# Two attention scores issued one behind the other on the two halves of TensorE's rows

## The reference

```python
def attend(qb):                      # 128 queries of each of 8 heads, head width 64
    s = einsum('bkgqd,bksd->bkgqs', qb, kh)      # 128 x 256 scores, no mask
    p = softmax(s, axis=-1)
    return einsum('bkgqs,bksd->bkgqd', p, vh)
o = lax.map(attend, q_blocks)        # 2 blocks of queries
o = rms_norm_2(o, out_gain)
mixed = concatenate([o_gla, o], -1)
h = h + mixed @ w_out                # then norm, router, top 2 of 64 experts, final norm
```

## Time and profile before

| | us |
|---|---|
| median of 3 runs | 1407.85 (1407.63 to 1408.08) |
| the profiled execution, its own time | 1395.12 |
| its span, first to last instruction | 1393.3 |
| PE busy | 1048.4 (75%) |
| DVE busy | 479.4 (34%) |
| ACT busy | 283.5 (20%) |

### The profile page before, as it was taken

One profiled execution on the slowest core, in us unless ns is written; L12 is line 12 of the kernel. 1 busy time (PEld: TensorE's weight loads), 2 busy tenths in 40 slices (PEclk: granted clock), 3 DMA queues, 4 the chain that ended last, 5 costly groups with the idle time before them and its releaser, 6 DMA issues.

```text
span 1393.3 us, 21666 instructions
## 1 busy us (share of the span) xinstructions
PE 1048.4 (75%) x9215; PEld 660.8 (47%) x9215; DVE 479.4 (34%) x1052; ACT 283.5 (20%) x610; POOL 36.1 (3%) x34
## 2 busy tenths in 40 slices
PE   8999999999999886675656766676665756757566
PEld 6857777878765542342323323233332423324232
DVE  4456785787954431221202212021120211212122
ACT  4334342544822111010001001010010110100000
POOL 0000101011102000000000000000000000000000
PEclk9999999999999998898889889798897988888898
DMA  8462255403575599999999999999999999999995
GB/s 308 136 242 70 70 203 181 155 31 131 183 313 236 211 377 426 425 428 425 427 426 425 428 426 425 428 426 425 428 427 425 428 425 427 427 425 427 427 424 239
DMA packets 69808, 463.75 MB, mean 333 GB/s; under 512 B 6722, under 2 KB 15108, under 8 KB 36356
## 3 DMA queue, kind: packets, MB, share of 16 engines
q1 hardware_dynamic: 68976, 460.48, 80.7%
q10 hardware_dynamic: 788, 2.66, 0.5%
HBM read 462.07 MB, written 1.05 MB: 332 GB/s over the span
## 4 chain that ended last, share of the span: by engine, by line
DMA 46%; PE 43%; DVE 6%; ACT 1%; issue 1%; SPq 1%; POOL 0%; DVEq 0%; ACTq 0%
DMA ring<-in_w_up 46%; PE bank L2226 14%; PE bank L1813 13%; PE bank L1796 5%; PE bank L1768 3%; PE bank L1842 2%; PE bank L1862 2%; PE bank L2246 1%; PE bank L1883 1%; SPq L552 1%; DVE ring_lo L1115 1%; PE bank L2300 1%; DVE ring_lo L1120 1%; PE bank L2208 1%; DMA res<-in_x 0%
## 5 line engine op out<-in xcount | busy, mean ns | idle before, releaser
L2226 PE MATMUL bank<-ring,expert_area 128*32 128x256 f32 x3968 | 323.3, 492 | 219.3 <-DMA ring<-in_w_up 219.0
L2226 PEld LDWEIGHTS bank<-ring,expert_area 128*32 128x32 f32 x3968 | 149.5, 137 | 385.8 <-DMA ring<-in_w_up 239.7
L1813 PE MATMUL bank<-ring_lo,xt_hi 128*128 128x512 f32 (+3 forms) x576 | 182.8, 386 | 0.6 <-DVE small L1305 0.4
L1650 DVE TENSOR_TENSOR expert_area<-expert_area,bank 128x128 f32<-128x128 f32 x64 | 18.3, 285 | 469.6 <-ACT expert_area L1008 469.6
L1008 ACT ACTIVATE expert_area<-bank 128x128 f32<-128x128 f32 x64 | 17.8, 278 | 618.0 <-PE bank L2226 618.0
L2246 PE MATMUL bank<-ring,consts 128*32 128x256 f32 x2016 | 121.8, 382 | 27.9 <-DVE consts L1652 27.9
L1813 PEld LDWEIGHTS bank<-ring_lo,xt_hi 128*128 128x128 f32 x576 | 104.1, 188 | 20.6 <-issue 3.7
L2246 PEld LDWEIGHTS bank<-ring,consts 128*32 128x32 f32 x2016 | 62.2, 109 | 69.2 <-DVE consts L1652 20.1
L1813 PE MATMUL bank<-ring_lo,xt_lo 128*128 128x512 f32 (+2 forms) x240 | 91.2, 380 | 0.0
L1796 PE MATMUL bank<-ring,xt 128*128 128x384 f32 (+1 forms) x192 | 75.7, 541 | 1.4 <-DVE xt L1079 0.8
L1656 DVE COPY consts<-bank 32x256 f32<-32x256 f32 x63 | 26.5, 421 | 132.7 <-PE bank L2246 132.7
(11 more groups left out here) (286 smaller groups left out, 1149.1 us busy)
## 6 DMA issues: line engine op xcount, KB each, us to landing
ring<-in_w_down SPq DMA_DIRECT2D x62, 2048.0 KB, 24.8
ring<-in_w_gate SPq DMA_DIRECT2D x61, 2048.0 KB, 18.3
ring<-in_w_up SPq DMA_DIRECT2D x60, 2048.0 KB, 22.8
ring<-in_moba_w_kv SPq DMA_DIRECT2D x4, 2048.0 KB, 8.0
ring<-in_moba_w_in SPq DMA_DIRECT2D x4, 2048.0 KB, 8.6
ring<-in_w_in SPq DMA_DIRECT2D x3, 2048.0 KB, 7.8
ring<-in_mla_w_uq SPq DMA_DIRECT2D x4, 1152.0 KB, 5.6
ring<-in_mla_w_o SPq DMA_DIRECT2D x2, 2048.0 KB, 7.9
```

What stands on the lines that cost most here:

```text
L1813: last = nc.tensor.matmul(dst, x[at], w[:, c, :], start=(piece == 0 and c == 0 and w is hi and x is xt_hi), stop=(piece == 1 and c == 3 an ...
L2226: last = nc.tensor.matmul(bank[2][SLOTS * j:SLOTS * j + SLOTS, 0:256], picked[:, c, SLOTS * i:SLOTS * i + SLOTS], both[:, :, c, j // 2, j ...
```

## The change

The body that issues a unit's scores becomes a function `score(u)`, unchanged in what it waits for and issues. For kinds "a" and "b" it is called at the same place as before. For kind "g" it is called at even steps only, for unit u and then at once for unit u+1. Every other instruction and wait stays where it was.

```diff
             def attention(kind, units, depth, scores, values, beside):
+                def score(u):
+                    h, tile = unit_of(kind, u)
+                    keys = keys_of(kind, tile)
+                    dst = score_bank_of(kind, u)
+                    if u >= 4:
+                        pe.wait_ge(probs_done, UNIT0[kind] + score_bank_before(kind, u) + 1)
+                    lhs, rhs = scores(h, tile, keys)
+                    causal = kind != "g"
+                    last = nc.tensor.matmul(dst[:, 0:keys], lhs, rhs, start=True, stop=not causal)
...
+                    last.then_inc(scores_in_psum, 1)
+
+                paired = kind == "g"
                 for u in range(units + depth + 1):
-                    if u < units:
...
-                        last.then_inc(scores_in_psum, 1)
+                    if u < units and not (paired and u % 2):
+                        score(u)
+                        if paired:
+                            score(u + 1)
                     m = u - depth
                     if 0 <= m < units:
                         pe.wait_ge(probs_done, UNIT0[kind] + m + 1)
```

More of the change, by code:

```diff
@@ L1831, in attention @@
             def attention(kind, units, depth, scores, values, beside):
-                for u in range(units + depth + 1):
-                    if u < units:
[L1834 to L1845, removed]
-                        last.then_inc(scores_in_psum, 1)
+                def score(u):
[7 more added lines that the diff above has]
+                    last = nc.tensor.matmul(dst[:, 0:keys], lhs, rhs, start=True, stop=not causal)
+                    if causal:
+                        last = nc.tensor.matmul(dst[:, keys - P:keys], ident_b[:], causal_b[:],
+                                                start=False, stop=True)
+                    last.then_inc(scores_in_psum, 1)
+                paired = kind == "g"
+                for u in range(units + depth + 1):
+                    if u < units and not (paired and u % 2):
+                        score(u)
+                        if paired:
+                            score(u + 1)
                     m = u - depth
```

## The result

The changed kernel takes 1389.85 us (median of 4 runs, 1389.73 to 1391.82) against 1407.96 before: ratio 0.9874, 95% interval 0.9857 to 0.9891. The forecast was 1404.6, a gain of 3.2 us; the gain is 18.1. But the two profiled executions are only 1395.12 - 1389.75 = 5.4 us apart. The 12.7 us between the profiled execution of the kernel before and its other runs, which the prediction carried along on both sides, have gone.

The account below looks back on a forecast made before the run. PE was taken to set the pace up to the expert load at 517.35 us, DMA after it. Five pair cycles x 0.57 = 2.85, less 0.1 and 0.12, plus 0.6, gave 3.2: 1407.85 to 1404.6 us, range 1402.9 to 1407.6.

Parts of the forecast that it names:

- Two scores at once for the price of one: In the attention on PE, a pair's second score overlaps the first and costs nothing, 0.03 us at most.
- Rival A: Attention scores start in program order, the odd one costing one instruction more: cycle 2.42, time 1405.9 us; chance 0.12.
- DVE's copy binds the cycle, 2.20: In the attention, the second V waits for DVE's copy of T: pair cycle 2.20 us, gain 0.57 a pair.
- Waits 0.1, scaling 0.12, tail 0.6: Attention: unit 5's score waits 0.1 us, DVE's scaling delays unit 9's V by 0.12, the end behind the last pair gains 0.6.
- All of it is handed on: A shift ahead of the expert gate load at 517.35 us moves the end by the whole 3.2 us.
- It stands 12.7 us under the median of the runs, and since that difference belongs to all of the program I subtract the same 3.2 from the median: Whole program: the profiled execution's 1395.1 goes to 1391.9, and the median's 1407.85 to 1404.6 us.
- Rival C: More PE idleness lowers the clock between 413 and 466 us; four falls cost 6.8, time 1411.4 us; chance 0.06.
- A stretch at 1.2 GHz loses 1.4 to 1.7, as at 473: A low-clock stretch of about 3.4 us, as at L2181, loses 1.4 to 1.7; sparing the 473 fall gains 1.4.

Follow-up runs that it names:

- after with the delay: The changed kernel with four idle matmuls (3.4 us) added between the attention and the projection that follows it; 1393.35 us.
- Before, filled: The kernel before with one idle matmul of 128 rows and 512 columns in PE's wait ahead of T0, the attention's first transpose; 1393.04 us.
- first pair only: The changed kernel with only units 4 and 5 issued as a pair, all later units as in the kernel before; 1392.91 us.
- before again: The kernel before, unchanged, built once more; 1407.62 us over 10 runs.
- delayed copy: The kernel before with four idle matmuls (3.4 us) added between the attention and the projection that follows it; 1410.93 us.
- fallen paired loop: The changed kernel with units 4 and 5 unpaired and pairs from unit 6 on, run again for a profile; 1400.7 us, the profiled run 1399.96.
- after with the longer gap: The changed kernel with four idle copies on ACT ahead of the first exponential, lengthening PE's wait ahead of T0, the first transpose; 1401.58 us.

## Why the prediction was wrong

- *Two scores at once for the price of one*: right. It is 0.63 from a pair to T, and on one half of the rows the cycle is 0.43 longer. Rival A, in program order, is out: the cycle is 2.17 and not 2.42, and the second score's first matmul runs from the first slice on. The rule of the Trainium skill that was set against it ("TensorE: Matmul & The Clock Gate", Part 3) doesn't describe these pairs.
- *DVE's copy binds the cycle, 2.20*: right, 2.17.
- *Waits 0.1, scaling 0.12, tail 0.6*: the first cycle took 2.25 (the wait, 0.08), the scaling cost nothing (pairs stay 2.17 apart at 419.5 and 421.6), and the tail gained 0.7 (4.05 instead of 4.76). With five cycles at 0.60 the attention gained 3.6 where the sum had 3.2.
- *All of it is handed on*: right. The load at 517.35 moved with it, the stretch behind that load is the same within 1.7 us in all profiles, and 3.4 us of added work cost 3.1 to 3.5.
- *"It stands 12.7 us under the median of the runs, and since that difference belongs to all of the program I subtract the same 3.2 from the median"*: this is the step that failed. The difference lay in the very stage that the change touches. The runs show it as 13.6 us of an attention at 1.2 GHz, in 46 of 52 runs of the kernel before by their times and mean clocks.
- *Rival C, the clock falls*: the mechanism was right and its side wrong. I let it strike after the change, for stretches of 3.4 us at 1.4 to 1.7 each. It was there already in most runs before, began right behind the wait ahead of T0, which I had not named, and lasted 34 us. The argument against it, that the waits of the attention bring none, came from the one execution that had escaped, and it counted the waits of 0.33 and 0.44 but not the one of 1.54.
- *A stretch at 1.2 GHz loses 1.4 to 1.7, as at 473*: too high for this place. In after the clock stays at 1.00 there, and still only 0.3 us is gained, because PE then waits 1.35 for DVE ahead of the first expert instead of 0.31 (before, then after):

```profile
476.51 3.87 PE L2226 MATMUL bank<-ring,expert_area 128*32 128x256 f32 x64 [0.31 <-DVE expert_area L1640]
471.86 3.87 PE L2231 MATMUL bank<-ring,expert_area 128*32 128x256 f32 x64 [1.35 <-DVE expert_area L1640]
```

From the group of 16 matmuls at 467.43 to this line it is 9.08 us in before, and 8.81 in after. Whether this fall comes isn't settled by the order of the scores: it is in the profiles of before and of after with the delay, and in none of the other three in which all six pairs overlap and the wait is 1.54 or filled.

The sum that the runs support: 14.4 us (1407.42 to 1393.04) for the clock, by the filled wait, and 3.2 (1393.04 to 1389.85) for the attention's own shortening: 17.6 of the 18.1. The other 0.5 is the difference between the two medians of before (1407.96 and 1407.42). The two come from different parts of the change: the first needs only unit 5's score right behind unit 4's, the second all six pairs.

What stays open is why a tenth of the runs of before escape. In the two profiles of the unpaired start that kept the clock, with the wait unfilled, the attention begins at 408.5 us; in the three that fell it begins at 406.8 to 407.7. The changed kernel begins at 407.1 to 407.7 in three profiles and keeps it. The times point the same way. Before, filled, and first pair only never fell, and six of their eight runs took 1392.3 to 1393.4, two 1395.0 and 1395.3; the profiled one at 1395.02 began at 408.56, that at 1392.36 at 407.10. All six runs of before that escaped took 1394.6 to 1395.1, none 1392 to 1394. So it seems that the unpaired order escapes only when the attention begins late. No run set that instant on purpose, so it isn't shown. Nor is it shown why one more score behind T0 is enough: it may be the work that it adds or the time at which it comes. How long a wait the changed kernel bears, between 1.54 and 2.76 on the weight loads, wasn't tried.

## What to carry to other kernels

When the profiled execution is further from the median than runs are from one another (here 12.7 us against 0.5), ask for the cause before you price a change, and look at its granted clock first: the profile may show the rare case. A wait on PE of a microsecond, ahead of work such as these scores and transposes, can cost many times its length, and a matmul that computes nothing, put into it, shows whether it does.

## What the runs showed of the hardware

- TensorE stays at 1.2 GHz for 34 us in which the profile has it busy for 2.00 of every 2.00 us, as long as its work is these scores, transposes and 64-column products. In all four profiles it rises in the tail, when no score is left: 7.7 us behind the load of the last score in before again, 8.7 in its delayed copy, 6.6 in the fallen paired loop and 3.9 in after with the longer gap. In the last it was back at 434.1, ahead of the transposes of the scaled output (435.89), among transposes and products like those of the loop. The Trainium skill, "TensorE: Matmul & The Clock Gate", Part 1, has the clock return with sustained activity; by these rows a PE that the profile calls busy throughout isn't enough.
- At 2.4 GHz the same loop holds the clock to its end (before filled, first pair only: 1.00 in every stretch). So at either level this loop keeps what it finds, and what stands at its start decides over 13.6 us.
- Two float32 scores on the two halves of the rows, each two instructions of 256 columns, take together the 0.63 us of one, and both begin within one slice of 0.05 us; on one half they add 0.43.
